# 96 slots an expert in place of 128 in the expert stage of a diffusion backbone

## What is computed

```python
def moe_swiglu(h, w_router, b_router, w1, w3, w2):
    logits = (h @ w_router).astype(jnp.float32) + b_router.astype(jnp.float32)
    top_v, top_i = lax.top_k(logits, TOP_K)                 # TOP_K = 2, 8 experts
    top_w = jax.nn.softmax(top_v, axis=-1)
    combine = jnp.sum(jax.nn.one_hot(top_i, N_EXPERTS) * top_w[..., None], axis=-2)
    out = jnp.zeros_like(h)
    for e in range(N_EXPERTS):
        out = out + combine[..., e:e + 1] * swiglu(h, w1[e], w3[e], w2[e])
    return out
```

## Time and profile before

| | us |
|---|---|
| runs | 1958.88, 1964.38, 1956.82 |
| median | 1958.88 |
| span of the profiled execution (first to last instruction) | 1955.9 |
| PE busy | 1923.2 (98%) |
| DVE busy | 1354.4 (69%) |
| ACT busy | 989.9 (51%) |
| stretch from 1200 to 1900 us: PE, DVE, ACT busy | 700.00, 631.76, 520.88 |

### The profile page before, as it was taken

One profiled execution on the slowest core, in us unless ns is written; L12 is line 12 of the kernel. 1 busy time (PEld: TensorE's weight loads), 2 busy tenths in 40 slices (PEclk: granted clock), 3 DMA queues, 4 the chain that ended last, 5 costly groups with the idle time before them and its releaser, 6 DMA issues.

```text
span 1955.9 us, 24019 instructions
## 1 busy us (share of the span) xinstructions
PE 1923.2 (98%) x9350; PEld 1540.7 (79%) x9350; DVE 1354.4 (69%) x1594; ACT 989.9 (51%) x1085; POOL 86.1 (4%) x127
## 2 busy tenths in 40 slices
PE   7999999999999999999999999999999999999997
PEld 6785666667788888878788988888888888888886
DVE  4663344478667646456355568989898989898996
ACT  4423333322522122234443376777777777777775
POOL 0050000010000001001100000000000000000000
PEclk9999999999999999999999999999999999999998
DMA  9412112255356557513243289999999999999990
GB/s 380 133 73 86 67 52 97 87 194 183 108 170 196 179 176 241 182 65 140 87 150 130 98 366 351 359 348 359 348 358 350 358 349 357 350 357 351 356 354 24
DMA packets 72835, 438.75 MB, mean 224 GB/s; under 512 B 9232, under 2 KB 10000, under 8 KB 28560
## 3 DMA queue, kind: packets, MB, share of 16 engines
q1 hardware_dynamic: 61056, 394.18, 53.4%
q0 software_dynamic: 11664, 43.00, 6.7%
HBM read 436.09 MB, written 1.05 MB: 223 GB/s over the span
## 4 chain that ended last, share of the span: by engine, by line
PE 93%; DVE 3%; ACT 2%; issue 1%; DMA 1%; SPq 0%; ACTq 0%; DVEq 0%
PE ps L1706 12%; PE ps L1708 12%; PE ps L1707 12%; PE ps L2146 8%; PE ps L2148 8%; PE ps L2147 8%; PE ps L1959 6%; PE ps L2160 4%; PE ps L2161 4%; PE ps L2166 4%; PE ps L1908 2%; PE ps L1867 2%; PE ps L1934 1%; PE ps L1837 1%; PE ps L1919 1%; PE ps L2130 1%
## 5 line engine op out<-in xcount | busy, mean ns | idle before, releaser
L1508 DVE TENSOR_TENSOR elo<-estage,ehi 128x2048 fp32r<-128x2048 f32 x264 | 604.6, 2291 | 74.8 <-ACT ehi L970 74.1
L970 ACT ACTIVATE ehi<-estage 128x2048 fp32r<-128x2048 f32 x264 | 505.8, 1917 | 119.3 <-PE ps L2148 71.0
L1706 PE MATMUL ps<-h_hi,whi 128*128 128x512 f32 (+1 forms) x960 | 368.6, 384 | 8.1 <-DVE h_lo L1132 4.6
L1708 PE MATMUL ps<-h_hi,wlo 128*128 128x512 f32 (+1 forms) x960 | 344.3, 359 | 0.0
L1707 PE MATMUL ps<-h_lo,whi 128*128 128x512 f32 (+1 forms) x960 | 344.1, 358 | 0.0
L2146 PE MATMUL ps<-ehi,xg_hi 128*128 128x512 f32 x704 | 282.8, 402 | 1.0 <-DVE elo L1508 1.0
L2148 PE MATMUL ps<-ehi,xg_lo 128*128 128x512 f32 x704 | 275.3, 391 | 0.0
L2147 PE MATMUL ps<-elo,xg_hi 128*128 128x512 f32 x704 | 275.0, 391 | 0.0
L1092 DVE TENSOR_TENSOR wlo<-stage,whi 128x2048 fp32r<-128x2048 f32 x79 | 180.7, 2288 | 98.2 <-ACT whi L704 98.0
L704 ACT ACTIVATE whi<-stage 128x2048 fp32r<-128x2048 f32 x79 | 150.8, 1909 | 164.0 <-PE ps L1708 163.9
L1706 PEld LDWEIGHTS ps<-h_hi,whi 128*128 128x128 f32 x960 | 181.1, 189 | 51.3 <-issue 12.8
(11 more groups left out here) (238 smaller groups left out, 2341.7 us busy)
## 6 DMA issues: line engine op xcount, KB each, us to landing
estage<-in_moe SPq DMA_DIRECT2D x264, 1024.0 KB, 5.2
stage<-in_split SPq DMA_DIRECT2D x79, 1024.0 KB, 5.4
gw<-in_mods POOLq DMA_DIRECT2D x80, 512.0 KB, 3.8
dw<-in_direct SPq DMA_DIRECT2D x36, 512.0 KB, 3.8
mw_a<-in_early SPq DMA_DIRECT2D x8, 512.0 KB, 8.2
mw_b<-in_early SPq DMA_DIRECT2D x8, 512.0 KB, 14.9
xT<-in_x SPq DMA_DIRECT2D x4, 512.0 KB, 5.4
gw<-in_cond_rows SPq DMA_DIRECT2D x1, 1024.0 KB, 17.7
```

The source lines that it names most:

```text
L970: act.activation(ehi[:, w % SPLIT, :], estage[:, w % STAGE, :], ACT.Copy).then_inc(S("e_hi_done"), 1)
L1508: dve.tensor_tensor(elo[:, w % SPLIT, :], estage[:, w % STAGE, :], ehi[:, w % SPLIT, :], ALU.subtract)\
L1706: pe.matmul(out, hi, rhs_hi, start=first, stop=False)
L1708: ins = pe.matmul(out, lo, rhs_hi, start=False, stop=last)
```

## The change

`SLOTS` is 96. All operands and outputs of the expert stage that have one slot per partition use partitions 0 to 95, those that have slots along the row are 96 long. The identity used in a turn of slot rows is 96 by 96. The experts' tokens beyond 96 are handled by up to two further passes (`PASSES` = 3: slots 96 to 191, 192 to 287) instead of one, behind the same branch, which now compares with 96; `posm` gets a third plane and `most_of_all` fills two of them. The semaphores of the extra passes get the number of their pass in the name.

```diff
-SLOTS = 128
+SLOTS = 96
+PASSES = -(-SEQ // SLOTS)
...
-    warm = fixed.take("warm", [P, 2])
+    warm = fixed.take("warm", [P, PASSES])
...
-    posm = htok.take("posm", [P, 2, 2, 2 * EXPERTS])
+    posm = htok.take("posm", [P, PASSES, 2, 2 * EXPERTS])
...
         with sp.If(most_r > SLOTS):
-            experts(1)
+            for p in range(1, PASSES):
+                experts(p)
...
-                    act.activation(xrow[:, f * 512:f * 512 + 512], ps[5 + f][:, :], ACT.Copy).then_inc(S("xrow"), 1)
+                    act.activation(xrow[0:SLOTS, f * 512:f * 512 + 512], ps[5 + f][0:SLOTS, :], ACT.Copy).then_inc(S("xrow"), 1)
...
-                    act.activation(xg_hi[:, x % 2, 4 * f:4 * f + 4, :], ps[5 + f][:, :].rearrange("p (k s) -> p k s", s=SLOTS), ACT.Copy)\
+                    act.activation(xg_hi[:, x % 2, 4 * f:4 * f + 4, :], ps[5 + f][:, 0:4 * SLOTS].rearrange("p (k s) -> p k s", s=SLOTS), ACT.Copy)\
...
-            step(dve.tensor_scalar(posm[:, 1, :, 0:EXPERTS], place, float(SLOTS), None, ALU.subtract))
+            for n in range(1, PASSES):
+                step(dve.tensor_scalar(posm[:, n, :, 0:EXPERTS], place, float(n * SLOTS), None, ALU.subtract))
...
-                    dve.tensor_scalar(sel[:, t, :], iota[:, :], one_of(posm[:, p, t, :], e, x), None, ALU.is_equal).then_inc(S("sel"), 1)
+                    dve.tensor_scalar(sel[:, t, :], iota[:, 0:SLOTS], one_of(posm[:, p, t, :], e, x), None, ALU.is_equal).then_inc(S("sel"), 1)
...
-                        dve.tensor_tensor(eu[:, cc % 2, :], et[:, cc % 2, :], ps[cc % 2][:, CW:2 * CW], ALU.mult).then_inc(S("eu"), 1)
+                        dve.tensor_tensor(eu[0:SLOTS, cc % 2, :], et[0:SLOTS, cc % 2, :], ps[cc % 2][0:SLOTS, CW:2 * CW], ALU.mult).then_inc(S("eu"), 1)
...
-                                ins = pe.matmul(ps[5 + f][:, :], sel[:, t, :], rows[:, t, f * 512:f * 512 + 512],
+                                ins = pe.matmul(ps[5 + f][0:SLOTS, :], sel[:, t, :], rows[:, t, f * 512:f * 512 + 512],
...
-                            ins = pe.transpose(ps[5 + f][:, k * SLOTS:(k + 1) * SLOTS], xrow[:, (4 * f + k) * P:(4 * f + k + 1) * P], ident[:, :])
+                            ins = pe.transpose(ps[5 + f][:, k * SLOTS:(k + 1) * SLOTS], xrow[0:SLOTS, (4 * f + k) * P:(4 * f + k + 1) * P], ident[0:SLOTS, 0:SLOTS])
...
-                    pe.transpose(ps[7][:, t * P:(t + 1) * P], sel[:, t, :].bitcast(F32), ident[:, :])
+                    pe.transpose(ps[7][0:SLOTS, t * P:(t + 1) * P], sel[:, t, :].bitcast(F32), ident[:, :])
...
-                    ins = pe.matmul(ps[7][:, SEQ:SEQ + 1], sel[:, t, :].bitcast(F32), one_of(comb[:, t, :], e, x), start=(t == 0), stop=(t == 1))
+                    ins = pe.matmul(ps[7][0:SLOTS, SEQ:SEQ + 1], sel[:, t, :].bitcast(F32), one_of(comb[:, t, :], e, x), start=(t == 0), stop=(t == 1))
...
-                    ins = pe.transpose(ps[2][:, pc % 2 * 256 + i * P:pc % 2 * 256 + (i + 1) * P], eu[:, pc % 2, i * P:(i + 1) * P], ident[:, :])
+                    ins = pe.transpose(ps[2][:, pc % 2 * 256 + i * SLOTS:pc % 2 * 256 + (i + 1) * SLOTS], eu[0:SLOTS, pc % 2, i * P:(i + 1) * P], ident[0:SLOTS, 0:SLOTS])
...
-                    o = ps[cc % 2][:, :]
+                    o = ps[cc % 2][0:SLOTS, :]
...
-                        pe.matmul(ps[3 + f][:, :], a_hi, hi[:, cols], start=first, stop=False)
+                        pe.matmul(ps[3 + f][0:SLOTS, :], a_hi, hi[:, cols], start=first, stop=False)
...
-                        pe.matmul(o, y_rows[:, kk // 2, at:at + P], selT[:, (x - 1) % 2, :], start=True, stop=False)
+                        pe.matmul(o, y_rows[0:SLOTS, kk // 2, at:at + P], selT[0:SLOTS, (x - 1) % 2, :], start=True, stop=False)
...
         with pe.If(most_r[0] > SLOTS):
-            last_scatter("fx")
-            experts(1)
+            for p in range(1, PASSES):
+                last_scatter(f"fx{p}")
+                experts(p)
```

More of the change, by code:

```diff
@@ L1008, in rows_hi @@
                 act.wait_ge(S("sc_full"), passed("sc_full", p) + e * 4 + 4 * x)
-                if p == 1:
-                    act.wait_ge(S("fx_sc"), 4)
+                if p >= 1:
+                    act.wait_ge(S(f"fx{p}_sc"), 4)
                 for f in range(2):
-                    act.activation(y_rows[:, 2 * f:2 * f + 2, 0:SEQ], ps[3 + f][:, :].rearrange("p (a c) -> p a c", a=2), ACT.Copy,
-                                   scale=w_slot[:, (x - 1) % 2:(x - 1) % 2 + 1]).then_inc(S("y_hi_e"), 1)
+                    act.activation(y_rows[0:SLOTS, 2 * f:2 * f + 2, 0:SEQ], ps[3 + f][0:SLOTS, :].rearrange("p (a c) -> p a c", a=2), ACT.Copy,
+                                   scale=w_slot[0:SLOTS, (x - 1) % 2:(x - 1) % 2 + 1]).then_inc(S("y_hi_e"), 1)
             def expert(e, v0, c_, x):
@@ L1033, in expert @@
                         act.wait_ge(used, passed("e_used", p) + v0 * STAGE + (SPLIT + w + 1))
-                        act.activation(et[:, cc % 2, :], ps[cc % 2][:, 0:CW], ACT.Silu).then_inc(S("et"), 1)
+                        act.activation(et[0:SLOTS, cc % 2, :], ps[cc % 2][0:SLOTS, 0:CW], ACT.Silu).then_inc(S("et"), 1)
                     if kind == "w" and c == 0:
@@ L1060, in experts, with last_rows_hi @@
             act.wait_ge(S("sc_full"), passed("sc_full", p) + 4 * EXPERTS)
-            if p == 1:
+            if p >= 1:
                 act.wait_ge(used, passed("e_used", p) + SPLIT + MOE_UNITS)
-        def last_rows_hi(tag):
-            act.wait_ge(S("e_used"), SPLIT + MOE_UNITS)
-            slot = w_slot[:, (EXPERTS - 1) % 2:(EXPERTS - 1) % 2 + 1]
+        def last_rows_hi(p, tag):
+            act.wait_ge(S("e_used"), passed("e_used", p - 1) + SPLIT + MOE_UNITS)
+            slot = w_slot[0:SLOTS, (EXPERTS - 1) % 2:(EXPERTS - 1) % 2 + 1]
             for f in range(2):
-                act.activation(y_rows[:, 2 * f:2 * f + 2, 0:SEQ], ps[3 + f][:, :].rearrange("p (a c) -> p a c", a=2), ACT.Copy, scale=slot)\
+                act.activation(y_rows[0:SLOTS, 2 * f:2 * f + 2, 0:SEQ], ps[3 + f][0:SLOTS, :].rearrange("p (a c) -> p a c", a=2), ACT.Copy, scale=slot)\
                     .then_inc(S(f"{tag}_hi"), 1)
@@ L1623, in _ @@
         with dve.If(most_r[0] > SLOTS):
-            last_rows_lo("fx")
-            last_adds("fx")
-            experts(1)
+            for p in range(1, PASSES):
+                last_rows_lo(f"fx{p}")
+                last_adds(f"fx{p}")
+                experts(p)
         last_rows_lo("fn")
@@ L2159, in down @@
                         cols = slice(i * D + f * 512, i * D + f * 512 + 512)
-                        pe.matmul(ps[3 + f][:, :], a_hi, hi[:, cols], start=first, stop=False)
-                        pe.matmul(ps[3 + f][:, :], a_hi, lo[:, cols], start=False, stop=False)
+                        pe.matmul(ps[3 + f][0:SLOTS, :], a_hi, hi[:, cols], start=first, stop=False)
+                        pe.matmul(ps[3 + f][0:SLOTS, :], a_hi, lo[:, cols], start=False, stop=False)
                     if i == 0:
@@ L2165, in down @@
                         cols = slice(i * D + f * 512, i * D + f * 512 + 512)
-                        ins = pe.matmul(ps[3 + f][:, :], a_lo, hi[:, cols], start=False, stop=last)
+                        ins = pe.matmul(ps[3 + f][0:SLOTS, :], a_lo, hi[:, cols], start=False, stop=last)
                 ins.then_inc(used, 1)
@@ L2183, in scatter @@
                         at = kk % 2 * P
-                        pe.matmul(o, y_rows[:, kk // 2, at:at + P], selT[:, (x - 1) % 2, :], start=True, stop=False)
-                        ins = pe.matmul(o, y_rows[:, 4 + kk // 2, at:at + P], selT[:, (x - 1) % 2, :], start=False, stop=True)
+                        pe.matmul(o, y_rows[0:SLOTS, kk // 2, at:at + P], selT[0:SLOTS, (x - 1) % 2, :], start=True, stop=False)
+                        ins = pe.matmul(o, y_rows[0:SLOTS, 4 + kk // 2, at:at + P], selT[0:SLOTS, (x - 1) % 2, :], start=False, stop=True)
                     ins.then_inc(S("sc_full"), 1)
@@ L2247, in last_scatter @@
                     at = kk % 2 * P
-                    pe.matmul(o, y_rows[:, kk // 2, at:at + P], selT[:, (EXPERTS - 1) % 2, :], start=True, stop=False)
-                    ins = pe.matmul(o, y_rows[:, 4 + kk // 2, at:at + P], selT[:, (EXPERTS - 1) % 2, :], start=False, stop=True)
+                    pe.matmul(o, y_rows[0:SLOTS, kk // 2, at:at + P], selT[0:SLOTS, (EXPERTS - 1) % 2, :], start=True, stop=False)
+                    ins = pe.matmul(o, y_rows[0:SLOTS, 4 + kk // 2, at:at + P], selT[0:SLOTS, (EXPERTS - 1) % 2, :], start=False, stop=True)
                 ins.then_inc(S(f"{tag}_sc"), 1)
```

38 lines of the change are left out of this document (19 added, 19 removed).

## The result

The changed kernel takes 1967.59 us (median of 11 runs, 1965.30 to 1974.02) against 1958.88 (11 runs, 1956.67 to 1966.26): 8.7 us more, ratio 1.0044 with a 95% interval of 1.0032 to 1.0056. The forecast was 1952, with a range up to 1963: the time lies outside the range, and the change is a loss where a gain was forecast. The profiled execution has a span of 1968.1 us, 12.2 above that of before.

What follows compares the result with a forecast made beforehand. PE's own stream was taken as the bound, DVE and DMA close behind. Terms -4.8 - 1.5 - 0.9 - 0.2 + 0.2 = -7.2 us, counted as -6.8, gave a 1949.1 us span, 1952.1 us measured; range 1938 to 1963.

Steps and rivals of the forecast that it cites:

- The big matmuls: 0: 3168 expert-stage matmuls with 512 moving columns: unchanged at 227 ns, cheaper load hidden behind the moving stream; 0 us.
- the rival: Expert stage's 3168 matmuls: fewer stationary columns make fp32r dearer, 3.2 us per ns, up to 1987 us; chance 0.06.
- My sign for it, a spacing over 232: 512-column matmuls starting over 232 ns apart, in place of 227, would show that narrower fp32r matmuls are dearer.
- The other rival: Big matmuls: the 14 ns above the 213.3 ns stream shrink with stationary width, 11 us less, 1941 us; chance 0.12.
- The turns and the selection: Expert stage's small instructions: hidden-row turns (L2130) -4.8 us, gathered-row turns (L2108) -1.5, selection's loads -0.9.
- two readings: L2130, hidden-row turns: moving side shortens both, -4.8 us (chosen), or only the matmul behind comes 27 ns sooner, -2.3.
- The -0.2 us for ACT and DVE: Smaller ACT and DVE copies: no gain except in the first chunks and the last turn, estimated at -0.2 us.
- the 0.4 held back for DMA: Expert stage: 0.4 us of the 7.2 us gain counted as lost, with DMA the tighter next limit.
- The second pass: Branch to extra passes: fullest expert has 80 tokens, below 96, so none runs; 0 us.
- The code behind the branch: 0: Extra-pass code behind the branch is longer but skipped in both kernels; taken as 0 us.
- The added step: most_of_all's one more dependent DVE step on the placement, ahead of the htok_lo copies PE waits for: +0.2 us.
- DVE and DMA as the next bound: Expert stage: with PE faster, DVE (632 us of work in 693) and DMA (359 GB/s) come next; both still fit.

Runs made afterwards that it cites:

- experiment 7: Changed code with 128 slots and two extra pass bodies (SLOTS = 128, PASSES = 3), against the kernel before: ratio 1.0025 (1.0014 to 1.0035).
- experiment 2: Changed kernel with fp32r matmuls back at 128 stationary columns (zeros in 96 to 127), transposes and selection at 96: ratio 1.0013 to before.
- 11: Kernel with 128-column fp32r stationaries, 96-column transposes and selection, both bodies, plus 40 unexecuted instructions in the skipped code: 1955.24 us against 1957.63 before, ratio 0.9988.
- experiment 6: Changed kernel with the code of one extra pass behind the branch in place of two: ratio 1.0036 to before (1.0023 to 1.0049).
- experiment 9: Changed kernel with 40 never executed instructions more at the end of the skipped code: ratio 1.0032 to before (1.0020 to 1.0045).
- 8: Kernel with 128 slots and two bodies, plus 12 never executed instructions at the end of the skipped code: ratio 1.0038 to before (1.0024 to 1.0052).

## Why the prediction was wrong

**The size of the change** is made of three parts: the stage (98.50 - 97.99) by 8 = 4.0 us, the added step 0.2, and the tail. The tail, last down matmuls to variance, took 10.6 to 13.2 us in the six profiles without the stall (mean 11.6) and 12.6 to 16.9 in the seven with it (mean 14.9): 3.3 us. The sum, 7.5, lies in the measured 6.3 to 11.0. The tail's share is the least certain: experiment 7 puts stall and added step at 4.9 us, experiments 2 and 11 differ by 5, but removing the stall from the changed kernel gave only 1.6 (experiment 6) and 2.4 (experiment 9).

**"The big matmuls: 0" failed.** That was the main step. I had argued that the moving side sets the pace and the cheaper load is hidden. The load is hidden (162 ns in a distance of 231), but the moving side doesn't set the pace alone: it is the same in both kernels, and each matmul got 3.8 ns dearer. By 404 matmuls and gathers an expert that is 1.5 us, by eight 12 us. With 12 us more the forecast of 1952 is 1964, outside my range already. 1.4 ns come from rows of 384 bytes, which the diff showed (`[P, 2, KD, SLOTS]`) and which I didn't price; 2.4 ns from the width. Why the engine is slower with either isn't known from these runs. I had the rival, at its place and with the right price of an ns (3.2 us), but gave it 0.06, because short loads are cheap. That argued from loads to matmuls, and no row showed an fp32r matmul below 128 columns. My sign for it, a spacing over 232, was also set too high: at 231.6 it already decides whether the change gains or loses. The other rival, that the 14 ns on top shrink with the width, had the wrong sign.

**The turns and the selection: the size right, the reason for L2130 half right.** The period closes: 404 by 3.77 ns is +1.52 us, measured is +0.50, so the small instructions gave back 1.02; the forecast had 0.9. A gathered turn went from 109 to 82 ns, by its moving side, as forecast. For a pair of turns L2130 I had two readings: the moving side shortens both (54 ns), or only the matmul behind them comes sooner by its cheaper load (27 ns). The starts show one of each. Between the two turns it is 85 ns in place of 108; from the second turn to the matmul behind 26 in place of 27; from this matmul to the next 291 in place of 314, although matmuls are 4 ns further apart. In the hybrid (experiment 2) the first two are 85 and 26 again, the last is 316. So the 57 ns come close to my 54 by luck: one turn's worth of moving side, and one load that my chosen reading had taken for hidden.

The -0.2 us for ACT and DVE and the 0.4 held back for DMA are too small for any of these runs to show.

**The second pass didn't run: right. "The code behind the branch: 0" failed.** I looked at whether it runs, not at where it puts the code behind it. Experiment 7 shows that the second body brings a stall, 8 and 9 that its place in the code decides where it falls and whether it comes at all; it takes 1.5 to 2.2 us. The page "Runtime: NRT & Kernel Launch" of the Trainium skill (Instruction fetch mechanics) says that code is fetched in blocks, in order, and that a taken branch to a place outside the blocks at hand must wait for its block; the stall that moves with the code agrees. Its size here is the trace's. The transfers in the traces fit too. In the changed kernel one of instructions (queue q8, 16 KB) starts at 1945.73 us and lands at 1946.65; PE stops at 1946.09 and goes on at 1948.17. In all 13 profiles such a transfer starts 0.7 to 1.1 us after the first small matmul, and in the seven with the stall PE goes on 1.3 to 1.5 us after its landing. The trace doesn't say whose code it is, so that PE waits for this one is likely, not shown. A second price may come with it. The first scatter comes on average 1.6 us later in the profiles with the stall, and the stretch from there to the variance takes 9.9 us in place of 8.1. The clock fell to the lower level in all 13 tails, 3.8 to 9.0 us after the last down matmuls with the stall (mean 6.4) and 6.9 to 9.5 without it (mean 7.9). That the hole in the small matmuls brings it down sooner is likely, but these ranges overlap.

**The added step: right** (0.18 us). **DVE and DMA as the next bound** never came up, since PE got no faster.

**The range** ended at 1963. With the dearer matmul at its real 3.8 ns and the stall priced, my own sum would have been -7.2 + 12.2 + 3.3 = +8.3 us. That the difference stays within 0.5%, which I had given 0.70, came true at 0.44% for another reason than mine, and on the other side. My own test of the mechanism failed clearly: the period of L2102 was to lie between 96.7 and 97.8 us and is 98.50.

## What to carry to other kernels

Where matmuls stream back to back, a few ns on each outweigh what is saved on the small instructions between them: before narrowing a stationary operand, time one such matmul at the new width, and in fp32r keep rows of 512 bytes on 512-byte lines (off them it cost about 4 ns a matmul here). Make only the transposes narrow, where the moving side is short, and leave the large ones full, with zeros. Code that never runs is not free if it stands in front of a short tail: look for a stall without a releaser behind the branch, and try to move it by padding. Whether that helped is seen in the trace first: in the time it was 2 to 5 us of 1960.

## What was unexpected in the hardware

- fp32r matmuls with 512 moving columns: 227.8 ns apart with a stationary operand of 128 columns on 512-byte lines, 232.6 with the same operand 128 bytes off the line, and, with narrower rows that start 512 bytes apart on the lines, 230.8 with 112 columns, 230.2 with 96, 233.1 with 80, although the load (188, 174, 162 and 148 ns, within the running stream) had time to spare in every case. The cause of the width's part was not found.
- A stall of 1.5 to 2.2 us without a releaser at a fixed place of PE's code behind a skipped body.
- A pair of transposes between large matmuls, a quarter narrower on the moving side: only the first gets shorter by it (108 to 85 ns), and the load of the matmul behind the pair isn't hidden (314 to 291 ns with 96 columns, 316 with 128).
- The clock's fall in the tail doesn't come at the same place in all executions: from the first scatter to the variance it took 6.9 to 10.9 us over 13 profiles; before's 6.9 was the shortest of all.
- The time up to the router's logits went from 1141.9 to 1149.1 us over these kernels, whose code up to there is all but the same. A profile's span can't be compared to better than that; an expert's period repeated to 0.02 us between kernels with the same expert stage.
